# A hand-scheduled two-block transformer kernel: bank waits, mLSTM parts, late columns, the last norm and the first loads put elsewhere

## The reference

```python
mod = silu(c) @ w_mod + b_mod                    # 6 x 1024: shifts, scales, gates
h = modulate(rms_norm(x, norm1_w), sh1, sc1)     # hc: the same for ctx
kc, vc = hc @ wi[:, K], hc @ wi[:, V]            # states s_f, s_b from the context
q, k, v, g, f = split_proj(h @ wi)
o = bidir_retention(rope(q), rope(k), v, a_f, a_b, s_f, s_b)
y = merge(sigmoid(h @ w_bg + b), ret_readout(o, g), fourier_mix(f)) @ w_out
x = x + g1 * y
x = x + g2 * conv_ffn(modulate(rms_norm(x, norm2_w), sh2, sc2))
x = rms_norm(x, final_norm_w)
```

```python
h = rmsnorm(x, norm1_g);  z = h @ w_in
merged = gate0 * (rwkv7(z_rw) @ p_rw) + gate1 * (mlstm(z_ml) @ p_ml)
x = x + merged @ w_out
x = x + peer(rmsnorm(x, norm2_g))
out = rmsnorm(x, final_g)
```

## Time and profile before

| | us |
|---|---|
| median of 3 runs | 1713.86 |
| lowest, highest | 1713.19, 1717.4 |
| profiled execution: own time | 1715.07 |
| profiled execution: span | 1713.2 |
| busy in the span: TensorE products | 1643.1 |
| VectorE, ScalarE, GpSimd | 1173.3, 802.0, 99.0 |

### The profile page before, as it was taken

How to read it: one execution, slowest core, us unless ns; L and a number is a source line. 1 busy time by engine, 2 the same in 40 slices (tenths; PEclk the granted TensorE clock), 3 DMA queues, 4 the chain that set the end, 5 groups by cost and what they waited for, 6 DMA issues and landing times.

```text
span 1713.2 us, 32554 instructions
## 1 busy us (share of the span) xinstructions
PE 1643.1 (96%) x12574; PEld 1505.7 (88%) x12574; DVE 1173.3 (68%) x2142; ACT 802.0 (47%) x1221; POOL 99.0 (6%) x124
## 2 busy tenths in 40 slices
PE   7999999999999999979999989999999999999997
PEld 2899978999999999878898877999999999999996
DVE  5646556777756769647498998666666666666665
ACT  2423436566644675324213993444444444444443
POOL 0000000022200001210052000000000000000000
PEclk9999899999999999999999999999999999999999
DMA  8765413545544443203333015555555555555553
GB/s 335 301 240 221 144 53 142 194 172 175 194 173 148 150 146 123 100 4 140 128 127 123 25 50 180 189 193 177 193 186 181 196 178 189 191 178 194 183 184 111
DMA packets 38538, 278.94 MB, mean 163 GB/s; under 512 B 4400, under 2 KB 4528, under 8 KB 5040
## 3 DMA queue, kind: packets, MB, share of 16 engines
q1 hardware_dynamic: 35136, 254.82, 41.5%
q0 software_dynamic: 2304, 16.78, 2.5%
q10 hardware_dynamic: 1008, 6.05, 1.0%
HBM read 276.58 MB, written 1.05 MB: 162 GB/s over the span
## 4 chain that ended last, share of the span: by engine, by line
PE 85%; DVE 8%; ACT 4%; issue 2%; DMA 1%; DVEq 0%; POOL 0%; ACTq 0%; POOLq 0%
PE ps L458 85%; DVE piece L1709 2%; ACT piece L1201 1%; DMA ring<-in_stream 1%; DVE pconst_sb L2453 1%; DVE cols L2453 1%; DVE late L2453 0%; DVE arena L1759 0%; DMA small<-in_cT 0%; ACT arena L1240 0%; DVEq L2453 0%; DVE arena L1795 0%; ACT L1236 0%; DVE arena L1776 0%; DVE arena L1828 0%
## 5 line engine op out<-in xcount | busy, mean ns | idle before, releaser
L458 PEld LDWEIGHTS ps<-h_r,piece 128*128 128x128 f32 x5664 | 699.0, 192 | 22.6 <-issue 10.4
L458 PE MATMUL ps<-h_r,piece 128*128 128x256 f32 x5664 | 708.5, 284 | 7.1 <-DVE piece L1709 4.9
L1709 DVE TENSOR_TENSOR piece<-ring,piece 128x1024 fp32r<-128x1024 f32 x434 | 533.0, 1236 | 255.6 <-ACT piece L1201 254.2
L1201 ACT ACTIVATE piece<-ring 128x1024 fp32r<-128x1024 f32 x432 | 452.5, 1056 | 367.4 <-PE ps L458 361.4
L458 PE MATMUL ps<-piece,late_r 128*128 128x512 f32 x1536 | 370.1, 391 | 1.4 <-DVE late_r L2475 1.4
L458 PEld LDWEIGHTS ps<-piece,late_r 128*128 128x128 f32 x1536 | 281.1, 188 | 55.4 <-issue 1.8
L2470 DVE TENSOR_TENSOR late<-late,arena 128x256 f32<-128x256 f32 x113 | 72.1, 638 | 117.6 <-ACT late L1667 117.6
L1667 ACT ACTIVATE late<-ps 128x256 f32<-128x256 f32 x113 | 43.5, 385 | 200.5 <-PE ps L458 200.5
L458 PE MATMUL ps<-arena,ring 128*128 128x256 f32 x480 | 110.5, 379 | 1.6 <-DVE arena L1776 1.6
L458 PEld LDWEIGHTS ps<-arena,ring 128*128 128x128 f32 x480 | 88.1, 190 | 12.3 <-issue 2.0
L458 PE MATMUL ps<-arena 64*64 64x64 f32 (+5 forms) x904 | 79.3, 292 | 9.6 <-DVE arena L2236 5.6
(11 more groups left out here) (324 smaller groups left out, 1701.9 us busy)
## 6 DMA issues: line engine op xcount, KB each, us to landing
ring<-in_stream SPq DMA_DIRECT2D x240, 1024.0 KB, 4.8
arena<-in_mod POOLq DMA_DIRECT2D x16, 1024.0 KB, 5.5
arena<-in_const ACTq DMA_DIRECT2D x1, 2256.0 KB, 10.2
arena<-in_const ACTq DMA_DIRECT2D x1, 1648.0 KB, 8.9
xres<-in_xT SPq DMA_DIRECT2D x1, 1024.0 KB, 12.1
arena<-in_xT SPq DMA_DIRECT2D x1, 1024.0 KB, 6.9
arena<-in_subk ACTq DMA_DIRECT2D x1, 1024.0 KB, 5.0
out<-arena SPq DMA_DIRECT2D x2, 512.0 KB, 2.7
```

Source lines behind the costliest of these rows:

```text
L458: mm_last[0] = nc.tensor.matmul(*args, **kw)
L1201: A(piece[:, 0, c % 3], ring[:, p % RING, s], ACT.Copy).then_inc(S["hi_ready"], 1)
L1709: TT(piece[:, 1, c % 3], ring[:, p % RING, s], piece[:, 0, c % 3].bitcast(F32), ALU.subtract).then_inc(S["lo_ready"], 1)
```

## The change

- SP sends x behind page 3 instead of ahead of it.
- VectorE clears a tile at the start; TensorE multiplies it with itself 13 times (256 columns, float32) before it waits for silu(c).
- The 8 products that add up `mcol` go behind page 3's products instead of page 5's.
- `wide` waits for the second bank at the first context product instead of at the start of the page.
- `late_columns(1)` goes from ahead of the third bg page to ahead of the second, into bank 3, and waits for the state copies instead of the rotations.
- `ym_r` gets a place of its own; its high part is made right after the last gate page on ScalarE, its low part after `gate_page(7)` on VectorE.
- Three products of `ones` (256 columns) stand between the first two `grams` and the products that wait for `x_init`.
- The last norm: `experts_done` counts halves of the tokens; the table of logarithm and exponential is loaded ahead of the wait; the root and reciprocal become Ln and Exp(-0.5 x); the scaling and the stores are cut into four of 512 columns.

```diff
@@ -172,7 +172,7 @@
         mg_r = pair("mg", 22016, 25088, 8)
         ffn_r = pair("ffn", 0, 10752, 22)
         y_r = pair("y", 10752, 12800, 4)
-        ym_r = pair("ym", 36864, 37888, 4)
+        ym_r = pair("ym", SPARE + 2048, SPARE + 1024, 4)
         mg2_r = pair("mg2", 4096, 6144, 8)
 
 
@@ -321,9 +321,9 @@
             page(0)
             page(1)
             page(2)
-            sp.dma_start(xres[:], t["xT"][:, 0]).then_inc(S["x_in"], 16)
             sp.wait_ge(S["start_sb"], START["sum0"])
             page(3)
+            sp.dma_start(xres[:], t["xT"][:, 0]).then_inc(S["x_in"], 16)
             sp.wait_ge(S["mod_used"], 1)
             page(4)
             sp.wait_ge(S["start_sb"], START["sum1"])
@@ -351,10 +351,12 @@
             pages_split(PAGE["first"] + RING, NPAGES - PAGE["first"] - RING, 2 * (WHOLE0 - SPLIT0))
 
 
-            for tt in range(2):
-                sp.wait_ge(S["fin_out"], tt + 1)
-                sp.dma_start(out[tt * P:(tt + 1) * P, :], fin[:, tt * 1024:(tt + 1) * 1024]).then_inc(S["out_dma"], 16)
-            sp.wait_ge(S["out_dma"], 32)
+            for n in range(4):
+                tt, c = n // 2, 512 * (n % 2)
+                sp.wait_ge(S["fin_out"], n + 1)
+                sp.dma_start(out[tt * P:(tt + 1) * P, c:c + 512],
+                             fin[:, tt * 1024 + c:tt * 1024 + c + 512]).then_inc(S["out_dma"], 16)
+            sp.wait_ge(S["out_dma"], 64)
 
 
         @block.gpsimd
@@ -477,15 +479,15 @@
 
 
                 turn(T)
-                if ctx:
-                    turn(T + 1)
                 for s in range(2):
                     c = piece_of(p) + s
                     piece_in(c)
                     w = [piece[:, q, c % 3].rearrange("p k m -> p (k m)").rearrange("p (k m) -> p k m", k=4) for q in range(2)]
                     for b, lhs in enumerate((h, hctx_r)[:1 + ctx]):
-                        if ctx_in and b == 1 and s == 0:
-                            pe.wait_ge(S["h_ready"], ctx_in)
+                        if b == 1 and s == 0:
+                            turn(T + 1)
+                            if ctx_in:
+                                pe.wait_ge(S["h_ready"], ctx_in)
                         for e in range(2):
                             half = slice(e * P, (e + 1) * P)
                             for kk in range(4):
@@ -635,6 +637,9 @@
                     m = nc.tensor.transpose(ps[:, 2, 2 * j:2 * j + 2], mrow[0:2, j * P:(j + 1) * P], ident[0:2, 0:2])
                 return m
 
+            pe.wait_ge(S["dch"], 1)
+            for _ in range(13):
+                mm(ps[:, 0, 0:256], h_tmp[:, 0, 0:P], h_tmp[:, 0, :], start=True, stop=True)
             pe.wait_ge(S["c_silu"], 1)
             for g in range(3):
                 for q in range(2):
@@ -644,13 +649,14 @@
                         m = mm(ps[0:2, 4 + g, :], csil[:, 4 * q + k, :], ring[:, p % RING, k // 2, 4 * (k % 2):4 * (k % 2) + 4, :],
                                start=q == 0 and k == 0, stop=q == 1 and k == 3)
                     m.then_inc(S["mod_used"], 1)
-                if g == 1:
+                if g == 0:
                     pe.wait_ge(S["pconst_in"], 16)
                     pe.wait_ge(S["start_sb"], START["sum1"])
                     for j in range(4):
                         for c in range(2):
                             mm(ps[:, 2, 24 + 2 * j + c:25 + 2 * j + c], mcol[c][:, j * P:(j + 1) * P], ones[:, 0:1],
                                start=True, stop=True)
+                if g == 1:
                     mod_columns(0)
             pe.wait_ge(S["start_sb"], START["stat"])
             mm(ps[:, 3, :], ones, sq1[:, 0, :], start=True, stop=True).then_inc(S["stat1"], 1)
@@ -665,7 +671,7 @@
             def late_columns(half):
 
                 pe.wait_ge(S["mod2_step"], 8 * (half + 1))
-                b, c = ((2, 32), (7, 0))[half]
+                b, c = ((2, 32), (3, 0))[half]
                 for j in range(16):
                     m = mm(ps[:, b, c + j:c + j + 1], mod_sum[half][:, j * P:(j + 1) * P], ones[:, 0:1], start=True, stop=True)
                 m.then_inc(S["mod2_mm"], 1)
@@ -698,10 +704,9 @@
 
             fm_page(PAGE["bg"], TURN["bg"], h)
 
+            pe.wait_ge(S["state_sb"], 2)
+            late_columns(1)
             for u in range(1, 6):
-                if u == 2:
-                    pe.wait_ge(S["qk_ready"], 4)
-                    late_columns(1)
                 fm_page(PAGE["bg"] + u, TURN["bg"] + u, h)
 
 
@@ -934,6 +939,8 @@
             pe.wait_ge(S["tok_sb"], 8)
             grams(0)
             grams(1)
+            turn(TURN["pm"] + 1)
+            idle_products(1, 3)
             pe.wait_ge(S["x_init"], 1)
             for q in range(2):
                 for k in range(8):
@@ -1159,8 +1166,8 @@
                             f.then_inc(S["piece_used"], 1)
                         mm(o, a[0], v[0], start=False, stop=False, skip_group_check=True)
                         m = mm(o, a[0], v[1], start=False, stop=end, skip_group_check=True)
-                if end:
-                    m.then_inc(S["experts_done"], 1)
+                    if end:
+                        m.then_inc(S["experts_done"], 1)
 
             pe.wait_ge(S["h_new"], 24)
             turn(T0 + EARLY)
@@ -1548,6 +1555,9 @@
             head_norm(m_dn, m_sq, 2, 4, (2, 3), 128, eps_ml, lambda: gate_page(3))
             for u in range(4, 8):
                 gate_page(u)
+            act.wait_ge(S["ym_ready"], 1)
+            for q in range(2):
+                A(ym_r[0][:, 2 * q:2 * q + 2, :], so[:, 2 * q:2 * q + 2, :], ACT.Copy).then_inc(S["part_hi"], 1)
             for n in range(8):
                 act.wait_ge(S["tok_mm"], n + 1)
                 A((atok, btok, ktok, vtok)[n // 2][:, n % 2, :], ps[:, 2 + n % 4, :], ACT.Copy).then_inc(S["tok_sb"], 1)
@@ -1574,9 +1584,6 @@
             for i in range(2):
                 act.wait_ge(S["u0_mm"], i + 1)
                 A(U0[:, i, :], ps[:, 4 + i, :], ACT.Copy).then_inc(S["u0_sb"], 1)
-            act.wait_ge(S["ym_ready"], 1)
-            for q in range(2):
-                A(ym_r[0][:, 2 * q:2 * q + 2, :], so[:, 2 * q:2 * q + 2, :], ACT.Copy).then_inc(S["part_hi"], 1)
             for i in range(2):
                 act.wait_ge(S["rw_mm"], i + 3)
                 A(yT[:, :, i * P:(i + 1) * P], ps[:, i, :].rearrange("p (j n) -> p j n", j=4), ACT.Copy).then_inc(S["rw_sb"], 1)
@@ -1681,13 +1688,15 @@
                 gelu(EARLY + u)
             act.wait_ge(S["a_ready"], P)
             act.dma_start(fgrow, t["fg"]).then_inc(S["fg_in"], 16)
-            act.wait_ge(S["experts_done"], 1)
+            nc.scalar.preload_act_table_set("natural_log_exp_and_others")
             for tt in range(2):
+                act.wait_ge(S["experts_done"], tt + 1)
                 A(at(1024 * tt, 1024).rearrange("p (a n) -> p a n", a=2), ps[:, 2 + 2 * tt:4 + 2 * tt, :], ACT.Square,
                   accum_out=fstat[:, tt:tt + 1]).then_inc(S["fin_sq"], 1)
-            for tt in range(2):
                 act.wait_ge(S["fin_sq"], tt + 1)
-                A(fstat[:, 2 + tt:3 + tt], fstat[:, tt:tt + 1], ACT.Sqrt, scale=1.0 / D, bias=eps6).then_inc(S["fin_root"], 1)
+                root = fstat[:, 2 + tt:3 + tt]
+                ac(A(root, fstat[:, tt:tt + 1], ACT.Ln, scale=1.0 / D, bias=eps6))
+                A(root, root, ACT.Exp, scale=-0.5).then_inc(S["fin_root"], 1)
 
 
         @block.vector
@@ -1781,6 +1790,7 @@
                         h[0][:, k, :].bitcast(F32), ALU.add, ALU.subtract).then_inc(S["h_new"], 1)
 
 
+            dv(V.memset(h_tmp[:, 0, :], 0.0))
             dve.wait_ge(S["c_silu"], 1)
             for q in range(2):
                 p = 2 * q
@@ -1871,7 +1881,7 @@
             def late_mod(half):
 
                 dve.wait_ge(S["mod2_mm"], half + 1)
-                b, c, m = ((2, 32, 16), (7, 0, 32))[half]
+                b, c, m = ((2, 32, 16), (3, 0, 32))[half]
                 return TT(mod[:, m:m + 16, 0], ps[:, b, c:c + 16], col("b_mod", m, 16), ALU.add)
 
             def weighted_keys(d):
@@ -2204,6 +2214,7 @@
                    zs[:, 8 + 2 * q:10 + 2 * q, :], ALU.mult)
             gate_page(6)
             gate_page(7)
+            lo_part(2, so, ym_r, "y_ready")
 
             dve.wait_ge(S["l_mm"], 1)
             for par in range(2):
@@ -2226,7 +2237,6 @@
                     ins = TT(x, x, ps[:, 4 + 2 * n + q % 2, 0:256].rearrange("p (a n) -> p a n", a=4), ALU.add)
                 ins.then_inc(S["x_sb"], 1)
 
-            lo_part(2, so, ym_r, "y_ready")
             dve.wait_ge(S["u0_sb"], 2)
             for n in range(4):
                 i, c = n // 2, n % 2
@@ -2500,9 +2510,10 @@
             for tt in range(2):
                 f = fin[:, tt * 1024:(tt + 1) * 1024]
                 dve.wait_ge(S["fin_root"], tt + 1)
-                dv(V.reciprocal(fstat[:, 2 + tt:3 + tt], fstat[:, 2 + tt:3 + tt]))
```

(6 more changed lines are left out.)

## The result

The changed kernel takes 1702.28 us (median of 4 runs, 1700.45 to 1704.93), the kernel before 1713.67 beside it (1713.19 to 1717.4): a ratio of 0.9925, 95% interval 0.9911 to 0.994, so faster by 11.4 us of the 15.45 forecast, inside the range. The profiled execution's own time is 1701.01, its span 1699.2 against 1713.2: 14.0 us shorter. The rows of the changed kernel come from that execution.

What follows compares the result with a forecast made beforehand. TensorE was taken to bound the kernel, with 85% of the chain; gains of 0.8 + 3.65 + 5.3 + 2.3 + 3.4 = 15.45 us from the median 1713.86 gave 1698.4 us, range 1694 to 1705.

Steps and rivals of the forecast that it cites:

- Start: x sent fourth, warm-up products and early column sums at the kernel's start: 0.8 us gained, bounds -1.2 and 1.3.
- I take 0.8, since the queue before page 8 has been drained further by then: Choice between page 8 landing at 37.3 (loses 1.2) and at 34.8 (gains 1.3), despite its later send near 30.0.
- The bounds (-1.2 to 1.3): At the kernel's beginning: page 8 landing at 37.3 loses 1.2 us, landing at 34.8 gains 1.3.
- Second bank: Five k and v pages: awaiting the bank at the context products removes 0.73 us each, 3.65 us; bounds 0 and 3.65.
- Late columns(1): Second lot of one-column sums moved behind page bg0: no 1.91 us wait, faster products; 5.3 us gained, bounds 1.9 and 7.0.
- the forecast's upper case (7.0): Moved second lot of one-column sums: 7.0 us gained if the clock doesn't fall at all.
- mLSTM parts and chunks: Parts made ahead of the chunk recurrence, idle products in the grams: 2.3 us gained in all, bounds -0.6 and 3.6.
- the bound of -0.6: Low bound for moving the mLSTM parts ahead of the chunk recurrence: 0.6 us lost.
- with an idle stretch shorter by 1.84 us the clock can stay at the upper level: Chunk recurrence: TensorE stays at the upper clock, so 4.67 us of products become 2.3.
- the clock falls in the chunks all the same: Rival: the chunk part gives 0 instead of 2.3, time 1700.7, as TensorE still waits for VectorE after every batch; chance 0.17.
- one long stretch without work: Chunk recurrence: the clock's fall was put down to TensorE's long idle time there, an argument against a fall after the change.
- End: Last norm after the final products: halved tokens, preloaded table, smaller scalings and stores; 3.4 us gained, bounds 3.0 and 3.8.

## Why the prediction was right, and where its terms were off

The direction and the range held; the sum was 15.45, the span gave 14.0 and the medians 11.4. Term by term:

**Start, +0.8 forecast, -0.95 measured: wrong in sign.** The sums cost their 1.95, as forecast, and page 3 came 0.45 earlier, not 0.7; that put page 8's send at 30.51, not near 30.0. The step that failed is "I take 0.8, since the queue before page 8 has been drained further by then": its flight became 0.7 shorter (6.58), not the 2 that a gain wanted. The bounds (-1.2 to 1.3) hold it.
What the runs add: with the old start the first row is at 39.1 to 39.3 in three kernels and at 40.76 in the kernel before, with the new start whole at 40.2 to 42.65 in seven. The means are 39.6 and 41.1, so as a set the edits cost some 1.5 us, and a single profile is uncertain by 1. With one of the three edits undone the row is at 41.51, 42.67 and 40.45: none of them alone brings the old start back. Three chains of nearly one length end there, and each came last in some profiles: over page 8 in seven of the 14, over TensorE's products up to the sums of squares in four, over the context's x in three.

Part of the scatter is the clock in page 3's products. Two kernels in which it stayed up there can be compared, by the chain, the one with the old start and then the one with the old bank waits and the new start:

```profile
16.84 10.75 PE ps L460 x24
...
27.61 7.05 DMA ring<-in_stream
```

```profile
16.50 12.44 PE ps L460 x40
...
28.96 6.98 DMA ring<-in_stream
```

Page 3 is there 0.34 earlier, the products with the sums among them take 1.69 longer, page 8 is sent 1.35 later, and the first row comes 1.26 later (40.55 against 39.29). Here the early sums are what costs. The warm-up's part isn't shown. The clock was down in page 3's products in 8 of 9 profiles with it and in 1 of 5 without. A longer idle time before them doesn't explain that: TensorE stood idle 2.9 to 3.1 us in three kernels without the warm-up and 3.85 in one with it, and the clock stayed up; it was 3.03 in the changed kernel and 2.26 in the one before, and the clock was down.

**Second bank, 3.65 forecast, 4.8 measured: the mechanism right, the size low.** The waits went, none turned into a wait for a piece. The upper bound, 5 x 0.73, wasn't one: each wait had 0.22 more behind it, which the chain doesn't list as waiting. It can be read from the page's period.

**Late columns(1), 5.3 forecast, 6.9 measured.** The wait of 1.91 and the slow products went; the clock then did not fall behind the second lot in this profile, the forecast's upper case (7.0). That was this execution: of the ten experiments with the lot whole in its new place, seven show a fall in or behind it (3.4 or 6.8 us at the lower level), the changed kernel and three experiments none. With the 1.7 of one fall the term is 5.2, and undoing it cost 5.8.

**mLSTM parts and chunks, 2.3 forecast, -1.8 measured: outside the bound of -0.6.** The steps up to the clock came as forecast: 1.8 won at VectorE's add, 0.3 lost at the tokens, 1.65 at the idle products (1.3 forecast: the six records took 1.56). The step that failed is "with an idle stretch shorter by 1.84 us the clock can stay at the upper level". The rival "the clock falls in the chunks all the same" came true, and dearer than it was priced: the clock fell 3.8 us behind the start of VectorE's first add (before, 1.7) and stayed down for 20.5 us, over nearly the whole rest of the serial chain. The lower bound took the clock to be at worst as before; the upper one, 3.6, leaves out 0.5 of its own terms (1.84 + 2.3 = 4.1 with nothing lost). The reason given for it, a wait for VectorE behind every batch, fits the runs: idle products that shortened most of the waits to 0.2 to 0.5 us removed the fall in one kernel and left 3.4 us of it in two others, while moving the parts back left it as it was. All three filled kernels lie below each of the eleven others, of which the lowest has 6.8. The "one long stretch without work", to which the prediction put the fall down, wasn't needed: it had shrunk from 2.69 to 0.97. How long the fall is without them varies: 20.5 to 24 us in six experiments of nine, 17.1, 13.7 and 6.8 in the others, 10.2 in the kernel before. Why it was shorter there can't be told from one profile. Nor is it shown whether the shorter waits or the wider products themselves keep the clock up: in the late columns it fell though TensorE never waited, and no run here has the one without the other.

**End, 3.4 forecast, 3.9 measured**, 0.1 above the bound: all steps as forecast, the last of the stores shorter than taken.

The sum came out near because the k and v and late-column terms ran over by 2.7 together while the start and the chunks fell short by 5.9. The profiled execution then had 1.5 of luck near 604 that no edit brought; the median of the runs stands 1.3 above it, the one of before 1.4 below its own. The four runs of the changed kernel go with the clock: 1700.45 at a mean of 0.992, 1701.01 at 0.990, 1703.55 at 0.989, 1704.93 at 0.988. The Trainium skill, "TensorE: Matmul & The Clock Gate" (the section on the HAM clock gate), says that the point of change isn't tied to the kernel's start and moves between runs; the fall between 598 and 621, which is in every profile, 3.4 or 6.8 us long, with no edit near it, agrees: it begins 2.5 to 5.0 us behind the start of the same eight records. They are four products, each over only four of the 128 rows, in the changed kernel

```profile
600.51 3.67 PE L460 MATMUL ps<-arena 4*128 4x512 f32 x8
```

and TensorE doesn't stand still in or behind them: from 600.5 to 604 the granted clock is 1.00, from 604 to 607.5 it is 0.51, with TensorE busy all the time.

## What to carry to other kernels

Await a result where it is used, not where its stage begins, and read the price from the stage's period: here five waits of 0.73 were worth nearly 0.96 each. Where a serial chain hands small batches back and forth between TensorE and VectorE, look at the granted clock before shortening the chain: one short product without use in most of the waits gave 4 us in 68, while the same kind of product in a stage that TensorE bounds cost all of its 1.65. A warm-up ahead of the first load makes the first products fast (3.60 instead of 5.75 us), which gains nothing where the next load is the bound. And work put ahead of what releases a load holds that load back by most of its length: the sums of 1.95 by 1.69.

## What the runs showed of the hardware

- Batches of 0.7 to 5 us of small products with waits of 0.8 to 1 us between them did not hold TensorE's clock: 0.51 over 21 us in which TensorE was busy for 17.69. With 17.01 us busy in the same window, products of 256 columns in most of the waits and 0.2 to 0.5 us left of these, it was 1.00.
- The whole lot of 16 one-column sums (32 records, 3.63 us) stands in 13 profiles twice; the clock fell in or behind 19 of the 26, though TensorE never stood still in them. In the one profile with the lots cut in halves (1.84 us) it fell behind none of the four. The four products over four rows near 600 (3.67 us) have a fall in or behind them in all 14 profiles.
- Page 3, 1 MB, took 4.67 to 5.03 us from send to landing in the nine profiles with x sent behind it, and 5.35 to 5.42 in the five with x sent ahead.
- The context's x, 1 MB, took 7.6 us from send to landing in the changed kernel and 10.1 in the experiment with the mLSTM parts put back, whose start is the same.
- A table load of 1.28 us hidden under the products left nothing behind: the square began 0.59 behind it, when its products were there, and the Ln ran in 0.29 right behind the square. Before, the root began 0.01 behind the load.
